# GpSimd adds the chunks of squares of a norm's root, in feed-forwards and mixers

## What is computed

```python
def _rmsnorm(x, g):
    xf = x.astype(jnp.float32)
    y = xf * lax.rsqrt(jnp.mean(xf * xf, axis=-1, keepdims=True) + EPS)
    return (y * g.astype(jnp.float32)).astype(x.dtype)
def _swiglu(h, wg, wu, wd):
    return (jax.nn.silu(h @ wg) * (h @ wu)) @ wd
...
    for i in range(DEPTH_2):
        h = _rmsnorm(x, ffn1_norm[i])
        x = x + 0.5 * _swiglu(h, ffn1_w_gate[i], ffn1_w_up[i], ffn1_w_down[i])
        h = _rmsnorm(x, mix_norm[i])
        x = x + _mixing(h, positions, w_in[i], w_out[i], fox_forget_bias[i], lbs[i],
                        hgrn_out_norm[i])
        h = _rmsnorm(x, ffn2_norm[i])
        x = x + 0.5 * _swiglu(h, ffn2_w_gate[i], ffn2_w_up[i], ffn2_w_down[i])
    return _rmsnorm(x, final_norm)
```

## Time and profile before

| | us |
|---|---|
| median of 3 runs | 2257.37 |
| the runs | 2255.13 to 2259.84 |
| the profiled execution | 2256.3 |
| its span, from the first instruction to the last | 2254.5 |

### The profile page before, as it was taken

The page is one execution under the profiler, slowest core; times in us unless marked ns, Lnnn a source line. Parts: engine busy times, 40 slices in busy tenths (PEclk is TensorE's granted clock), DMA queues, the critical chain, the costliest instruction groups (busy, mean ns, idle before and its releaser), DMA issues. The chain is left out here.

```text
span 2254.5 us, 33241 instructions
## 1 busy us (share of the span) xinstructions
PE 2130.4 (94%) x13753; PEld 1468.4 (65%) x13753; DVE 1124.7 (50%) x1759; ACT 770.8 (34%) x1029; POOL 3.0 (0%) x6
## 2 busy tenths in 40 slices
PE   6978889999999999999997999999999999999999
PEld 4757634443333333334434888998888888998888
DVE  4764512111111111112215876788865874788874
ACT  3553221111001100111114554546544653546543
POOL 0000000000000000000000000000000000000000
PEclk8989989999999999999998999999999999999999
DMA  9443779999999999999996655444655665434652
GB/s 373 163 172 123 303 307 429 430 430 430 430 430 430 430 429 430 430 430 430 430 428 199 194 193 181 150 131 132 206 198 176 195 196 188 143 121 149 195 198 75
DMA packets 200254, 626.02 MB, mean 278 GB/s; under 512 B 13200, under 2 KB 150224, under 8 KB 164304
## 3 DMA queue, kind: packets, MB, share of 16 engines
q1 hardware_dynamic: 197536, 622.72, 71.6%
q10 hardware_dynamic: 2608, 1.72, 0.3%
HBM read 623.36 MB, written 1.05 MB: 277 GB/s over the span
## 5 line engine op out<-in xcount | busy, mean ns | idle before, releaser
L2070 DVE TENSOR_TENSOR w_low<-ring,w_high 128x2048 fp32r<-128x2048 f32 x168 | 384.0, 2290 | 170.0 <-ACT w_high L2065 170.0
L2065 ACT ACTIVATE w_high<-ring 128x2048 fp32r<-128x2048 f32 x168 | 320.3, 1910 | 175.1 <-PE bank L2409 139.4
L2404 PE MATMUL bank<-h_both,w_high 128*128 128x512 f32 x1344 | 322.5, 392 | 0.0
L2404 PEld LDWEIGHTS bank<-h_both,w_high 128*128 128x128 f32 x1344 | 246.6, 188 | 48.9
L1828 PE MATMUL bank<-ring,ut 128*64 128x512 f32 x1024 | 243.2, 624 | 31.7 <-DMA ring<-in_exp_w_dram 31.6
L1800 PE MATMUL bank<-ring_odd,xt 128*64 128x512 f32 x1024 | 224.7, 596 | 0.9 <-DMA ring_odd<-in_exp_w_dram 0.9
L1800 PE MATMUL bank<-ring,xt 128*64 128x512 f32 x1024 | 223.3, 594 | 0.3 <-ACT xt L1882 0.3
L1886 ACT ACTIVATE sg<-glu 128x512 f32<-128x512 f32 x32 | 20.2, 630 | 545.4 <-DVE glu L1949 545.4
L1828 PEld LDWEIGHTS bank<-ring,ut 128*64 128x64 f32 x1024 | 71.6, 142 | 187.3 <-issue 127.3
L1965 DVE SCALAR_TENSOR_TENSOR xT<-bank,mod,xT 128x256 f32<-128x256 f32 x128 | 55.6, 480 | 248.5 <-PE bank L1842 248.5
L2409 PEld LDWEIGHTS bank<-h_both,w_low 128*128 128x128 f32 x1344 | 167.6, 188 | 7.0
(11 more groups left out here) (552 smaller groups left out, 2658.8 us busy)
## 6 DMA issues: line engine op xcount, KB each, us to landing
ring<-in_exp_w_dram SPq DMA_DIRECT2D x64, 2048.0 KB, 26.7
ring_odd<-in_exp_w_dram SPq DMA_DIRECT2D x64, 2048.0 KB, 27.9
ring<-in_exp_w_dram SPq DMA_DIRECT2D x128, 1024.0 KB, 25.1
ring<-in_ffn_w_gate_dram SPq DMA_DIRECT2D x44, 1024.0 KB, 5.5
ring<-in_ffn_w_up_dram SPq DMA_DIRECT2D x44, 1024.0 KB, 5.4
ring<-in_ffn_w_down_dram SPq DMA_DIRECT2D x44, 1024.0 KB, 4.9
ring<-in_w_in_dram SPq DMA_DIRECT2D x36, 1024.0 KB, 5.5
ring<-in_ada_w_dram SPq DMA_DIRECT2D x24, 1024.0 KB, 12.1
```

The costliest lines, as they stand in the source:

```text
L2065: nc.scalar.activation(w_bufs[0][u % BUFS], ring2[:, u % RING2, :], ACT.Copy).then_inc(high2, 1)
L2070: nc.vector.tensor_tensor(w_bufs[1][u % BUFS], ring2[:, u % RING2, :], w_bufs[0][u % BUFS].bitcast(F32), ALU.subtract).then_inc(low2, 1)
L2404: return nc.tensor.matmul(b[:, :], w_parts[0][:, at:at + P], moving.rearrange("p a t -> p (a t)"), start=start, stop=False, skip_group_che ...
```

## The change

In a feed-forward the three additions go to GpSimd, unchanged in shape, in a stream of their own that waits for all four pairs of squares and for nothing of VectorE. In a mixer GpSimd adds the eight chunks to two, in three instructions (pairs 0 and 2, pairs 1 and 3, then the two results), ahead of its memset, and TensorE multiplies two chunks and no longer eight. The matmul waits for GpSimd's third addition in both.

```diff
-                for c in range(DC):
-                    if c % 2 == 0:
-                        pe.wait_ge(sem(f + "squares"), c // 2 + 1)
-                    ins = nc.tensor.matmul(total, ones, squares[:, c, :], start=(c == 0), stop=(c == DC - 1))
+                pe.wait_ge(sem(f + "squares_added"), 3)
+                for c in range(2):
+                    ins = nc.tensor.matmul(total, ones, squares[:, c, :], start=(c == 0), stop=(c == 1))
                 ins.then_inc(sem(f + "total"), 1)

-            def add_squares(dve):
-                dve.wait_ge(sem(f + "squares"), 4)
+            def add_squares(gps):
+                gps.wait_ge(sem(f + "squares"), 4)
                 for i, n in enumerate((4, 2, 1)):
                     if i:
-                        dve.wait_ge(sem(f + "squares_added"), i)
-                    nc.vector.tensor_tensor(squares[:, 0:n, :], squares[:, 0:n, :], squares[:, n:2 * n, :], ALU.add
+                        gps.wait_ge(sem(f + "squares_added"), i)
+                    nc.gpsimd.tensor_tensor(squares[:, 0:n, :], squares[:, 0:n, :], squares[:, n:2 * n, :], ALU.add
                                             ).then_inc(sem(f + "squares_added"), 1)
...
+            if begins:
+                @S.block.gpsimd
+                def _(gps):
+                    add_squares(gps)
...
                 for n in span:
                     during(n)
-                    if n == 0:
-                        add_squares(dve)
...
             @S.block.gpsimd
             def _(gps):
+                for j in range(2):
+                    gps.wait_ge(sem(f + "squares"), j + 3)
+                    nc.gpsimd.tensor_tensor(squares[:, 2 * j:2 * j + 2, :], squares[:, 2 * j:2 * j + 2, :], squares[:, 2 * j + 4:2 * j + 6, :], ALU.add
+                                            ).then_inc(sem(f + "squares_added"), 1)
+                gps.wait_ge(sem(f + "squares_added"), 2)
+                nc.gpsimd.tensor_tensor(squares[:, 0:2, :], squares[:, 0:2, :], squares[:, 2:4, :], ALU.add).then_inc(sem(f + "squares_added"), 1)
                 gps.wait_ge(sem(f + "total"), 1)
                 nc.gpsimd.memset(at_[:, :, :, :], 0.0).then_inc(sem(f + "cleared"), 1)
```

## The result

The changed kernel takes 2277.72 us (median of 4 runs, 2276.04 to 2280.17) where the kernel before, run beside it, takes 2257.74 us (4 runs, 2255.13 to 2259.84). The ratio is 1.0094, with a 95% interval of 1.0081 to 1.0106: 20 us slower by the medians, 21 by the ratio. The prediction had the sign, with 2267 us, and half of the size; the result lies 5.7 us above the upper end of its range.

A forecast was written before the change was run, and what follows sets the result against it. TensorE's stream was taken to bound the kernel. Feed-forwards 9.4 us and mixers 0.6 us made 10.0 us on the profiled 2256.3 us, 2267.4 against the median of 2257.37, given as 2267 us; range 2254 to 2272.

The forecast's parts named there:

- What bounds the kernel, and what a feed-forward can give: Whole kernel: TensorE's stream is the time; feed-forwards can give only its waits for VectorE's additions, 1.69 us together.
- The price of an addition: GpSimd: 2.25 ns an element, so 2.3, 1.15 and 0.6 us for a feed-forward's three additions.
- Exclusion: GpSimd additions and VectorE low parts run one at a time; feed-forward sums 9.4 us later in all; chance 0.55.
- unit 3's high part is ready at 1562.77, so VectorE is out of the way: Second feed-forward: no VectorE low part then delays GpSimd's additions, which end at 1563.0, sum 2.0 us later.
- In a feed-forward nothing gives this back, as TensorE's stream is full behind it and a stall is pure addition: Feed-forwards: the sums' delays, 9.4 us in all, add to the time in full.
- The mixers' gain: Mixers: TensorE comes 2.45 us early but can use only 0.2 us each, 0.4 us in all; the rest idles.
- The mixers' loss: Mixers: additions delay chunks 6 and 7 and TensorE's first units by 0.5 us; 0.3 us net each, 0.6 in all.
- No exclusion: Rival: GpSimd's additions run undisturbed, feed-forward waits go (1.69 us), mixers give 0.4: 2255.3 us; chance 0.20.
- sharing: Rival: while GpSimd and VectorE both read, each goes at half speed, 3.5 us together: 2260.9 us; chance 0.13.
- GpSimd is much dearer: Rival: additions at 2.70 ns or with a start of their own, under exclusion: 2272 us; chance 0.07.
- The mixers keep their matmuls' time: Rival: chain behind the root less tight, and no exclusion; 6.6 us gained, 2250.8 us; chance 0.05.

The follow-up runs named there:

- vector_early: Kernel before, with VectorE's feed-forward additions moved ahead of the low part of unit 2: 2255.03 us, ratio 0.9994 (0.9985 to 1.0004).
- memsets: Changed kernel, each of GpSimd's three additions in a feed-forward replaced by a memset of 1536 elements: 2254.29 us, ratio 0.9997 (0.9988 to 1.0007).
- filled: Changed kernel, with 24 matmuls of thrown-away result on TensorE ahead of its feed-forward wait for the additions: 2269.19 us, ratio 1.0060 (1.0043 to 1.0077).
- mix_root_first: `mix_only` with the mixers' root taken ahead of unit 4's high and low parts: 2253.72 us, ratio 0.9991 (0.9981 to 1.0000).
- root_first_pe: Kernel before, mixers' root ahead of unit 4's parts, all eight chunks still summed on TensorE: 2257.26 us, ratio 1.0007 (0.9997 to 1.0016).
- mix_only: Kernel before with the change in the mixers alone, feed-forwards as before: 2256.51 us, ratio 1.0005 (0.9995 to 1.0015).
- one_add: Changed kernel, GpSimd making only the first feed-forward addition and TensorE summing four chunks: 2259.55 us, ratio 1.0014 (1.0003 to 1.0024).
- mix_late: `mix_root_first`, but GpSimd starts only when all squares are there and makes two additions, not three: 2255.60 us, ratio 0.9988 (0.9979 to 0.9997).

## Why the prediction was half right

**What bounds the kernel, and what a feed-forward can give:** right. TensorE's stream is the time, and the 1.69 us of waits were all that was there; `vector_early` takes them away, and the first feed-forward, which had 1.14 us of them, gets 1.0 us shorter.

**The price of an addition:** right. 2.3, 1.15 and 0.6 us were put in, 2.27, 1.14 and 0.58 us came out in the turns (0.72 for the last where it met nobody). The middle between "the reads in turn" and "all three in turn" was a choice, and that it happened to be the value was luck. The Trainium skill's figure ("GPSIMD Engine Reference", Performance versus the Vector engine), 4497 ns for 2048 elements, is 2.2 ns each, and the trace agrees with 2.27 us for 1024.

**Exclusion:** right as a mechanism, and the memsets in the additions' place (`memsets`) confirm it. Its size was the first step that failed. I predicted the four sums to be 2.7, 2.0, 2.7 and 2.0 us later; TensorE's waits for them grew by 1.7, 3.85, 2.3 and 3.8 us, 11.6 us and not 9.4. In the first and the third I was 1.0 and 0.4 us high. In the second and the fourth the error is one sentence: "unit 3's high part is ready at 1562.77, so VectorE is out of the way". The high part at 1560.85 is not unit 3's but that of the unit behind it. Unit 3's high part was done at 1554.15 + 3.71 = 1557.86 in the kernel before, so its low part was ready to go all along,

```profile
1554.15 3.71 ACT L2065 ACTIVATE w_high<-ring 128x2048 fp32r<-128x2048 f32 x2
```

and in the trace of after it stands between the second and the third addition, at 1565.01 to 1567.16. That is 2.15 us in each, which is more than the whole gap of 1.8 us between 2.0 and 3.8. I had also written that it doesn't matter whether an addition gets in between two low parts, since the sum of all is the same. That holds only if the number of low parts ahead of the last addition is the same, and under turns it isn't: each of the three additions lets one more low part past if one is ready.

**"In a feed-forward nothing gives this back, as TensorE's stream is full behind it and a stall is pure addition":** this is the second step that failed, and the larger. A stall was more than an addition. TensorE's clock fell to the lower level at three of the four, and another 6.3 us went in the feed-forwards: about 2 us a place, for 2.3 to 4.1 us of idle time. `filled` is the run that shows it, for 5.3 us of the 6.3. The prediction has no term for the clock, though it forecast idle spells of 2 to 4 us. With 6 us more for the clock, and 2 us for the turns, the sum of 2267 would have been 2275, within 3 us of the result; the mixers' loss, below, is another 1.2 us.

**The mixers' gain:** right in its mechanism; its 0.2 us each is too small to be measured. 4.9 us of matmuls went, and the profile of after has 4.6 us of new idle time ahead of levels 0 and 3, in both mixers together, released by ScalarE and VectorE, where the prediction put it. That the root is what holds them was only argued from the earlier trace rows; `mix_root_first` with `root_first_pe` shows it.

**The mixers' loss:** too small. 0.3 us each was predicted, 1.5 and 0.3 us came. In the first mixer I let the additions delay TensorE's first units by 0.5 us. Unit 1 began 9.43 us after unit 0 where it had been 8.29 us, 1.14 us later. Nearly all of it, 1.03 us, was lost by the last matmul of unit 0, on the low parts of chunks 6 and 7, which were caught by two additions and not one; the low part of 3.37 us behind them cost 0.1 us. In the second mixer the same additions find TensorE about 1.5 us later against its chunks, and most is covered. So the term is right at one place and 1.2 us short at the other. (In the four other runs with these mixers, `mix_only`, `memsets`, `filled` and `one_add`, the first was 1.0 to 1.6 us longer than before, the second 0.1 to 0.4.) `mix_late` moves the additions behind the chunks, and the wait goes.

**The rivals.** "No exclusion" and "sharing" fall with the ends in turns. "GpSimd is much dearer" had the nearest time, 2272 us, by a price of an addition that isn't so. "The mixers keep their matmuls' time" falls with the new idle time ahead of the levels and with `mix_only`, which is no faster than before. Nothing in the list was the clock, and so the range ended too low.

What stays open is the difference between the first feed-forward and the third. The one keeps the full clock behind 2.83 us of idle time, the other loses it behind 2.27 us. What came before isn't the same. From 1204 to 1222 us TensorE waited for 4.1, 3.2 and 3.6 us, and its clock was at 0.50 until shortly before the additions (1.00 from 1226 to 1228 us); ahead of the third it had been at 1.00 and without a wait:

```profile
1222.00:1224.00 2.00, 2.00 (x11) 2.00 (x11) 1.93 (x6) 2.00 (x5) 0.00 (x0) 0.50 0.80 262
...
1744.00:1748.00 4.00, 4.00 (x38) 4.00 (x37) 4.00 (x6) 3.60 (x5) 2.13 (x1) 1.00 0.00 0
```

No run varies this, so whether it matters isn't shown. Nor do the second feed-forward's rows add up to the last microsecond: the unit behind the sum and the matmul of ones are 2.6 us longer, and the stage is 1.5 us longer than its wait explains. Of the 1.1 us between, 0.4 came back ahead of the sum, where TensorE waited 0.9 us for a chunk and not 1.3; the rest stays open.

## What to carry to other kernels

Before work goes to GpSimd "because it is idle", look at what VectorE does in the same window: if it reads two operands from SBUF, an addition on GpSimd and it take turns (one read a single tensor and was held up all the same, see below), each hand-over costs the whole of the other's instruction, and one large operation loses less than three small ones that depend on each other. Price a stall in a full TensorE stream with the granted clock in mind, here half as much again as the stall. And when a shorter piece of work saves nothing, look for the chain that the waits behind it name, and move its first link; the saving was there to be had, 2 to 3 us against the kernel before, once the root came ahead of two splits.

## What the runs showed of the hardware

- A waiting GpSimd addition gets its turn behind VectorE's current instruction, with one exception in these traces: 1557.33 to 1561.72 behind a low part that ended at 1559.45. In the third feed-forward it asked at 1745.87, 0.05 us after a low part had begun (1745.82 to 1748.11), and was passed over: the next low part ran too, to 1750.31, and only then the 2.27 us of the addition. That is 6.71 us for it, and 10.8 us for the three. The same addition takes 6.72 us in `one_add`.
- The profile counts the wait for the turn as busy time, on both engines. Of GpSimd's 50.6 us about 26 are work by the lengths of the turns (16.0 for the feed-forwards' additions, 6.8 for six of 1.14 us in the mixers, 3.0 for the memsets of the earlier trace rows); the rest is nearly all waiting. And VectorE's low parts have a mean of 2370 ns for 2.29 us alone. A mean that rises where nothing of the instruction changed is a trace of this.
- Two operands on VectorE aren't needed for it. In `mix_late` a TENSOR_SCALAR of VectorE with 128x4 elements and one tensor to read, 0.155 us long in the changed kernel, took 2.37 us in both mixers, until GpSimd's addition of 1024 elements was over. It is one instruction in two places, and no run varies it:

```profile
1417.47 2.37 DVE L3086 TENSOR_SCALAR one_less<-lower 128x4 f32<-128x4 f32 x1
```

- A memset is exempt: three of 1536 elements ran in 4.28 us beside low parts at 2.23 us each.
- Matmuls whose result nobody reads kept the granted clock at 1.00 over a stall of 4 us, with 1.28 us of it left idle (`filled`), and the kernel was 6 to 8 us faster for them.
